# Two mixers reordered and the opening rebuilt in a two-block transformer kernel

## What is computed

```python
h = rmsnorm(x, mix_norm[l])
z = h @ w_in[l]
q, k, v, f_logit, gate_in, rec_in = jnp.split(z, split_points, axis=-1)
log_f = jax.nn.log_sigmoid(f_logit.astype(jnp.float32) + b_forget[l].astype(jnp.float32))
att = forgetting_attention(...)   # softmax(q k^T * scale + c_q - c_k, causal) v, c = cumsum(log_f)
rec = causal_depthwise_conv(rec_in, conv_w[l], conv_b[l])
rec = rg_lru(rec, w_a[l], b_a[l], w_x[l], b_x[l], lru_lambda[l])
lru_out = rec * jax.nn.gelu(gate_in, approximate=True)
x = x + jnp.concatenate([att, lru_out], axis=-1) @ w_out[l]
```

```python
q, k, v, g = jnp.split(x @ w_in, [H * dk, 2 * H * dk, 2 * H * dk + H * dv], axis=-1)
q = retention_rotate(...); k = retention_rotate(...) * (dk ** -0.5)
y = retention_chunkwise(q, k, v)          # ((q k^T) * decay mask) v, over chunks
y = head_rms(y).reshape(B, T, H * dv)
return (jax.nn.silu(g) * y).astype(x.dtype) @ w_out
```

## Time and profile before

| | |
|---|---|
| median of 3 runs | 2901.12 us (2900.29 to 2904.52) |
| the profiled execution's own time | 2903.57 us |
| its span | 2901.6 us |
| mean granted TensorE clock | 0.974 |
| TensorE busy | 2732.4 us, 94% |
| VectorE, ScalarE, GpSimd busy | 61%, 49%, 4% |

### The profile page before, as it was taken

One profiled execution on the slowest core, in us unless ns is written; L12 is line 12 of the kernel. 1 busy time (PEld: TensorE's weight loads), 2 busy tenths in 40 slices (PEclk: granted clock), 3 DMA queues, 4 the chain that ended last, 5 costly groups with the idle time before them and its releaser, 6 DMA issues.

```text
span 2901.6 us, 47985 instructions
## 1 busy us (share of the span) xinstructions
PE 2732.4 (94%) x19842; PEld 2461.7 (85%) x19842; DVE 1766.3 (61%) x2117; ACT 1421.8 (49%) x1872; POOL 115.2 (4%) x187
## 2 busy tenths in 40 slices
PE   4789999989999999997998999999999999999999
PEld 4669999978898888887897888889978888888887
DVE  3445588865655656568765656556546665555655
ACT  3435467644545445457323545445335455454544
POOL 0000000000000000000211000000000000000000
PEclk9889999999999999999999999999999999999999
DMA  5207599945543555553301555555535555543453
GB/s 168 73 5 249 176 320 358 332 158 188 169 150 121 199 188 182 188 174 105 129 4 42 193 190 188 189 189 179 178 116 181 188 167 192 193 147 129 167 189 130
DMA packets 377581, 491.96 MB, mean 170 GB/s; under 512 B 18872, under 2 KB 337760, under 8 KB 377408
## 3 DMA queue, kind: packets, MB, share of 16 engines
q1 hardware_dynamic: 365280, 479.23, 49.7%
q0 software_dynamic: 2192, 7.73, 0.8%
q10 hardware_dynamic: 9936, 2.47, 0.4%
HBM read 488.35 MB, written 1.05 MB: 169 GB/s over the span
## 4 chain that ended last, share of the span: by engine, by line
PE 87%; DVE 6%; ACT 4%; issue 1%; POOL 1%; ACTq 1%; DMA 0%; POOLq 0%; DVEq 0%
PE bank L348 20%; PE bank L347 11%; PE bank L327 9%; PE bank L328 9%; PE bank L329 9%; PE acc L327 7%; PE acc L329 7%; PE acc L328 7%; PE bank L2592 1%; ACT w_hi L292 1%; PE acc L588 1%; DVE X L499 1%; DVE w_lo L297 1%; ACTq L874 1%; PE bank L2569 1%
## 5 line engine op out<-in xcount | busy, mean ns | idle before, releaser
L297 DVE TENSOR_TENSOR w_lo<-raw,w_hi 128x2048 fp32r<-128x2048 f32 x360 | 824.1, 2292 | 536.8 <-ACT w_hi L292 536.4
L292 ACT ACTIVATE w_hi<-raw 128x2048 fp32r<-128x2048 f32 x360 | 687.9, 1911 | 269.0 <-PE acc L329 234.3
L348 PE MATMUL bank<-act_both,w_hi 128*128 128x512 f32 x2560 | 654.6, 392 | 0.0
L348 PEld LDWEIGHTS bank<-act_both,w_hi 128*128 128x128 f32 x2560 | 465.2, 189 | 82.8
L347 PEld LDWEIGHTS bank<-act_both,w_lo 128*128 128x128 f32 x2560 | 349.2, 190 | 25.0
L327 PE MATMUL acc<-w_hi,mix_hi 128*128 128x512 f32 x928 | 364.4, 393 | 2.3 <-DVE mix_lo L3017 1.2
L329 PE MATMUL acc<-w_hi,mix_lo 128*128 128x512 f32 x928 | 362.5, 391 | 0.0
L328 PE MATMUL acc<-w_lo,mix_hi 128*128 128x512 f32 x928 | 362.3, 390 | 0.0
L347 PE MATMUL bank<-act_both,w_lo 128*128 128x256 f32 x2560 | 357.0, 282 | 0.0
L722 ACT ACTIVATE scratch<-bank 128x256 f32<-128x256 f32 x320 | 122.2, 385 | 429.2 <-PE bank L348 422.8
L327 PE MATMUL bank<-act_both,w_hi 128*128 128x256 f32 x1032 | 298.5, 289 | 21.0 <-DVE act_both L2844 8.4
(11 more groups left out here) (501 smaller groups left out, 3889.9 us busy)
## 6 DMA issues: line engine op xcount, KB each, us to landing
raw<-in_ffn_w_gu SPq DMA_DIRECT2D x176, 1024.0 KB, 5.1
raw<-in_ffn_w_down SPq DMA_DIRECT2D x88, 1024.0 KB, 4.9
raw<-in_ml_w_in SPq DMA_DIRECT2D x24, 1024.0 KB, 5.3
raw<-in_rt_w_in SPq DMA_DIRECT2D x24, 1024.0 KB, 5.1
raw<-in_w_up SPq DMA_DIRECT2D x20, 1024.0 KB, 7.7
raw<-in_w_gate SPq DMA_DIRECT2D x19, 1024.0 KB, 7.1
raw<-in_w_down SPq DMA_DIRECT2D x18, 1024.0 KB, 6.8
moe_raw<-in_w_down SPq DMA_DIRECT2D x14, 1024.0 KB, 6.9
```

Source lines behind the costliest of these rows:

```text
L292: act.activation(w_hi[0:rows, slot, 0:size], raw[0:rows, slot, 0:size], ACT.Copy).then_inc(hi_made, 1)
L297: dve.tensor_tensor(w_lo[0:rows, slot, 0:size], raw[0:rows, slot, 0:size], w_hi[0:rows, slot, 0:size].bitcast(F32), ALU.subtract).then_inc ...
L348: return pe.matmul(bank[b][:, :], w_hi[:, slot, w], act_both[:, k, :], start=k == 0, stop=k == KT - 1)
```

## The change

The opening: the constants are loaded in two pieces (the identity first). Of the vectors ScalarE's queue loads only `mix_norm`, which TensorE turns alone. The other vectors and the forget columns go to SyncE's queue behind the first three panels, the narrow weights and biases to GpSimd's queue behind the first norm. The splits of the first three panels move into the norm (`between`). GpSimd, not VectorE, clears `qz` (and `kz`).

The first mixer: panels come in the order v, rec, gate, q, k, and the output panels in the order 2, 3, 0, 1 (the recurrence's rows first). The forget columns are 24 products with a 72-row left side, the cumulative sum is a scan on VectorE, and both q and k carry it in unused rows of `qz` and `kz`, so that the product L986 and `cT` go away. The reciprocal is replaced by `a*a + 1` times the tanh. The scores write to the four `acc` banks, and `probs` has four buffers. The gates, the recurrence and the heads stand between panels.

Retention: the scores of all heads stand behind panel g0, the y and turns between the panels g1 to g7.

The core of the diff (TensorE's order in both mixers, the opening, and the parts of ScalarE's and VectorE's programs that wait for each other):

```diff
-            act.dma_start(con[:, :], consts).then_inc(consts_loaded, 16)
-            act.wait_ge(setup_dve, 2)
-            for dst, src in small_loads:
-                act.dma_start(dst, src).then_inc(small_loaded, 16)
-            act.wait_ge(small_loaded, 16 * len(small_loads))
-            act.activation(narrow_hi[:, :, :], narrow[:, :, :], ACT.Copy).then_inc(setup_act, 1)
-            for p in range(RING):
-                act_split(act, p, 1, None)
+            act.dma_start(con[:, 0:P], consts[:, 0:P]).then_inc(consts_loaded, 16)
+            act.dma_start(*vec_loads[0]).then_inc(mix_loaded, 16)
+            act.dma_start(con[:, P:], consts[:, P:]).then_inc(consts_loaded, 16)
+            act.wait_ge(cleared, 1)
+            act.activation(silu_out[:, 0, 0:32], exponent[:, :], ACT.Square)
 
...
-            dve.memset(exponent[:, :], -0.5).then_inc(setup_dve, 1)
-            dve.memset(rows_in[:, VEC_TILES - 1, :], 0.0).then_inc(setup_dve, 1)
-            dve.wait_ge(small_loaded, 16 * len(small_loads))
-            dve.wait_ge(setup_act, 1)
-            dve.tensor_tensor(narrow_lo[:, :, :], narrow[:, :, :], narrow_hi[:, :, :].bitcast(F32),
-                              ALU.subtract).then_inc(setup_dve, 1)
-            dve.wait_ge(setup_pe, 1)
-            dve.tensor_copy(vecs[:, :], acc[0][:, 0:VEC_TILES * P]).then_inc(setup_dve, 1)
-            for p in range(RING):
-                dve_split(dve, p, p)
+            dve.memset(exponent[:, :], -0.5).then_inc(cleared, 1)
+            dve.memset(rows_in[:, VEC_TILES - 1, :], 0.0).then_inc(cleared, 1)
+            dve.memset(f_w[:, :, :], 0.0).then_inc(cleared, 1)
+            dve.wait_ge(mix_turned, 1)
+            dve.tensor_copy(vecs[:, 0:MIX_ROWS], acc[3][:, 0:MIX_ROWS]).then_inc(mix_ready, 1)
+            dve.wait_ge(mix_ready, 1)
...
-            pe.wait_ge(consts_loaded, 16)
-            pe.wait_ge(small_loaded, 16 * len(small_loads))
-            pe.wait_ge(setup_dve, 2)
-            for j in range(VEC_TILES):
-                last = pe.transpose(acc[0][:, j * P:j * P + P], rows_in[:, j, :], ident)
-            last.then_inc(setup_pe, 1)
...
+            pe.wait_ge(consts_loaded, 32)
+            pe.wait_ge(mix_loaded, 16)
+            pe.matmul(acc[3][:, 0:MIX_ROWS], rows_in[0:MIX_ROWS, 0, :], ident[0:MIX_ROWS, 0:MIX_ROWS], start=True,
+                      stop=True).then_inc(mix_turned, 1)
+            pe.wait_ge(mix_ready, 1)
...
+                if j == RING:
+                    sp.wait_ge(cleared, 3)
+                    for dst, src in vec_loads[1:]:
+                        sp.dma_start(dst, src).then_inc(vec_loaded, 16)
+                    for dst, src in f_loads:
+                        sp.dma_start(dst, src).then_inc(f_loaded, 16)
                 sp_panel(sp, p, p % RING, [(col_view(p % RING), w[:, :, at:at + PW])])
...
+            att_pool.wait(pool, "k_cleared")
+            pool_cross(pool, c)
...
+            for dst, src in narrow_loads:
+                pool.dma_start(dst, src).then_inc(narrow_loaded, 16)
...
+                if h >= 4:
+                    att_act.wait(pe, ("exp", h - 4))
+                for t, cols, at in ((1, T, 0), (0, P, T)):
+                    pe.matmul(acc[h % 4][:, at:at + cols], qz[:, h, t * P:t * P + P], kz[:, h, 0:cols], start=True, stop=False)
+                    last = pe.matmul(acc[h % 4][:, at + cols - P:at + cols], ident, C("neg_qk"), start=False, stop=True)
...
+            project("rec", 0)
+            b = result("f")
...
+            project("rec", 1)
+            project("gate", 0)
+            project("gate", 1)
+            for j in range(4):
...
+                att_dve.wait(pe, ("conv", j))
...
+            project("q", 0)
+            project("k", 0)
+            project("q", 1)
+            for h in range(4):
+                scores(h)
+            project("k", 1)
+            turn(0)
+            turn(1)
+            wait_evacuated(pe, N["v", 0])
+            wait_evacuated(pe, N["v", 1])
+            values(0)
+            for h in range(4, 8):
+                scores(h)
+            turn(2)
+            turn(3)
+            values(1)
+            turn(4)
+            turn(5)
+            values(2)
+            out_rows(0)
+            turn(6)
+            turn(7)
+            values(3)
+            out_rows(1)
...
+            projected("gate", 1)
+            act.wait_ge(narrow_loaded, 16 * len(narrow_loads))
+            act.activation(narrow_hi[:, :, :], narrow[:, :, :], ACT.Copy).then_inc(narrow_high, 1)
+            act.wait_ge(narrow_low, 1)
...
+            att_act.done(act.activation(lru_t[:, :, :], lru_t[:, :, :], ACT.Sqrt), "sqrt")
+            projected("q", 1)
+            for h in range(4):
+                exps(h)
+            lru_high(0)
+            lru_high(1)
+            projected("k", 1)
+            turned_copy(0)
+            turned_copy(1)
+            exps(4)
+            high(0)
+            turned_copy(2)
+            exps(5)
+            turned_copy(3)
+            high(1)
+            exps(6)
+            exps(7)
+            turned_copy(4)
+            turned_copy(5)
+            high(2)
+            act_split(act, (c.p + 13) % RING, loads(c.p + 13), E["out", 0])
+            turned_copy(6)
+            turned_copy(7)
+            high(3)
...
-                own(dve.tensor_scalar(lru_r[:, :, :], lru_t[:, :, :], 1.0, None, ALU.add))
-                own(dve.reciprocal(lru_r[:, :, :], lru_r[:, :, :]))
...
+            att_act.wait(dve, ("powers", 3))
+            own(dve.tensor_tensor(lru_r[:, :, :], lru_a[:, :, :], lru_a[:, :, :], ALU.mult))
+            att_dve.done(dve.scalar_tensor_tensor(lru_t[:, :, :], lru_r[:, :, :], 1.0, lru_t[:, :, :], ALU.add, ALU.mult),
+                         "square")
+            ahead("q", 0)
+            ahead("k", 0)
+            att_act.wait(dve, "sqrt")
+            own(dve.tensor_tensor(lru_i[:, :, :], lru_i[:, :, :], lru_t[:, :, :], ALU.mult))
+            for j in range(4):
+                last = dve.tensor_tensor_scan(lru_r[:, j, :], lru_a[:, j, :], lru_i[:, j, :], 0.0, ALU.mult, ALU.add)
+            att_dve.done(last, "u")
...
+            for j in range(2, 8):
+                project("v", j)
+            for j in range(8):
+                project("q", j)
+            project("g", 0)
+            for h in range(4):
+                scores(h)
+            project("g", 1)
+            for j in range(8):
+                wait_evacuated(pe, N["v", j])
+            retained(0)
+            project("g", 2)
+            retained(1)
+            turn(0)
+            project("g", 3)
+            retained(2)
+            turn(1)
+            project("g", 4)
+            retained(3)
+            project("g", 5)
+            turn(2)
+            project("g", 6)
+            project("g", 7)
+            turn(3)
```

More of the change, by code:

```diff
@@ L465, in act_cross @@
                 x_sum(0)
+            if between:
+                between(0)
             if norm:
@@ new lines, in dve_att @@
+            ahead("q", 0)
[5 more added lines that the diff above has]
+            att_dve.done(last, "u")
+            att_dve.wait(dve, "u")
+            for j in range(2):
+                wait_evacuated(dve, N["gate", j])
+                lru_out(j)
@@ L2221, in pe_rt, with turn @@
+            def turn(h):
+                rt_dve.wait(pe, f"scaled{h}")
+                for i in range(2):
+                    b = result("turn", h, i)
                     for m in range(2):
```

908 lines of the change are left out of this document (516 added, 392 removed).

## The result

The changed kernel takes 2850.31 us (median of 4 runs, 2847.51 to 2854.70), the kernel before 2902.82 on the same chip (4 runs). The ratio is 0.9821, with a 95% interval of 0.9804 to 0.9838: 1.8% faster, some 52 us. The profiled execution took 2848.55 us (span 2846.8), 55.0 less than that of before. The forecast was 2845.

What follows compares the result with a forecast made beforehand. TensorE, busy 94% of the span, was taken as the bound, so gains come from its idle or slow time: 48.3 us through the first mixer (opening's 24.7 included) plus 7.5 in retention, 55.8, giving 2845 us; range 2830 to 2862 (8 in 10).

Steps and rivals of the forecast that it cites:

- The opening: Kernel start: first norm's diagonal moves from 38.03 to 13.2 us, the second panel's product from 47.8 to 23.1; gain 24.7 us.
- What was put at nothing: Opening: moved vector, forget, panel 3 and narrow loads, and GpSimd's clearing of `qz` and `kz`, were taken to cost nothing.
- 1.9: First mixer: TensorE's wait for q0's bank, 5.3 us of ScalarE's work against 3.4 of gate products; 1.9 us.
- 7.2: First mixer: TensorE out of work from 93 us until the second turned copy near 100, before the first values; 7.2 us.
- 1.5: First mixer: wait because turned copies of heads 2 and 3 stand between the exponentials of heads 4 and 5; 1.5 us.
- 2.8: First mixer: wait because turned copies of heads 4 and 5 stand behind the exponentials of 6 and 7; 2.8 us.
- 2.0: First mixer: wait because turned copies of heads 6 and 7 stand behind the last split, which waits for the first output panel; 2.0 us.
- clock: First mixer: products at 1.2 GHz around one long wait and three short ones; taken at 3 us.
- Retention: Retention's heads: 6.4 us of TensorE idle time plus about 1 of slow clock go; gain 7.5, bounds 0 and 8.5.
- The rule on table changes: Skill's 1.38 us drain beside each 1.28 us ScalarE table load; four changes before the first exponential add 5.5 us, sum 2851.
- the slower one: Rival, chance 0.02: GpSimd's narrow loads hold ScalarE before the gates, with 36 us free; slower than 2901, 2908 at 14 us each.
- Relays overlap better: Rival, chance 0.17: ScalarE and VectorE overlap, so half of the 15.4 us of mixer waits and no clock loss; 2834.

Runs made afterwards that it cites:

- e1: Changed kernel with ScalarE again issuing the vectors, forget and narrow weights itself and waiting for them before the first norm's squares; 2863.66 us, ratio 0.9859.
- e7: Changed kernel with the first three panels' splits again ahead of the first norm on both engines, small loads as changed; 2857.89 us, ratio 0.9841.
- e4: Changed kernel with, on ScalarE alone, turned copies of heads 0 and 1 ahead of k1's copy and split and the recurrence's copies; 2845.41 us, ratio 0.9793.
- e10: The changed kernel itself run again, nothing edited, on the same chip and in the same rounds; 2848.01 us, ratio 0.9812 against the kernel before.
- e8: Changed kernel with GpSimd's ten narrow loads made three times, each behind the last's landing, ScalarE and VectorE waiting for the third; 2857.15 us, ratio 0.9831.
- e5: Changed kernel with the first mixer's heads taken ahead of what doesn't feed them, on VectorE, ScalarE and TensorE; 2838.86 us, ratio 0.9769.
- e6: Changed kernel with heads first on three engines, plus narrow weights split behind rec 1 and q1's split behind the gates; 2836.66 us, ratio 0.9755.
- e2: Changed kernel with the five retention programs of the kernel before; 2857.78 us, ratio 0.9835.
- e3: Changed kernel with ScalarE splitting the narrow weights behind panel rec 1 and doing q1's split behind the four gates; 2844.27 us, ratio 0.9792.

## Why the prediction was right, and where it was off

- **The opening**: 24.7 us predicted, 47.79 to 23.07 measured, 24.7. The second panel's product starts when VectorE's low half is made, at 23.0; I had 23.1. One premise was wrong and cost nothing: the first half's products, which I had at the slow clock, follow every 0.12 us from 17.4 on. e1 and e7 show that the loads' wait and the splits ahead of the norm are two conditions, of 14.6 and 8.8 us.
- **What was put at nothing**: right. TensorE doesn't wait between 23 and 59 us. The allowance of 3 us for a narrow load was too much: four took 3.50. GpSimd's clearing cost nothing either; the root came at 13.5.
- **The first mixer's waits**: 15.4 predicted, 12.9 measured (1.76 of q0's bank, then 0.38 + 0.67 + 5.52 + 0.60 + 2.07 + 1.88). Against the terms: 1.9 was 1.76; 7.2 was 6.57; 1.5 was 0.60; 2.8 was 2.07; 2.0 was 1.88. All five stand where the orders put them, the third below the 1 us that I had as the least. I read the 2.5 us too much as ScalarE and VectorE overlapping a little more than end to end; no run separates it. The *clock* was taken at 3, and cost about 3.7: some 1.4 at 65 us (between 65.0 and 68.3 the products follow every 0.21 us in place of 0.12), and 2.3 between 100.2 and 106.2, where the same work took 3.7 us in e4. From the second panel's product to the mixer's end there are 118.3 us; less waits and clock that leaves 101.7 of work, for which I had 100.2. Most of the 1.5 can be read as restarts behind waits, as under retention: the last product ahead of a wait is drawn 0.07 to 0.16 us longer than such products follow one another, and over the eight waits that is 1.2 (an estimate from the timeline). Errors of opposite sign made 141.7 meet 141.3. And the 190 from which I counted was the end of a window; the next norm's first product stood at 189.4 before, from which the forecast would have been 47.7 and not 48.3. No run puts the old mixer back: its 23.3 us are read from the two traces, and what the new order, the missing product with `cT`, the reciprocal, the forget columns and the banks each give is not shown.
- **Retention**: the term that was mis-sized. 7.5 predicted with a bound of 8.5; 9.2 from the sine on in every trace. The idle time is 6.4; the clock is not 1 but about 1.8 (the last turn 1.79 us for 1.04, and the first output products slow until 2143.9); another 1.0 is a remainder, and most of it can be read as idle time that the wait column doesn't hold, since a matmul's end is modelled and the tail of the last product ahead of a wait counts as busy. The Trainium skill has this too ("Perfetto Trace Analysis", "Tensor Engine Instruction (MATMUL, LD_WEIGHTS)": the end of a TensorE instruction is estimated, not measured). The five waits of the stage before each stand behind a product drawn 0.16 us longer than such products follow one another (0.27 for 0.11, 0.59 for 0.43), which makes 0.8; this is an estimate, no run measures a tail. The mistake was to set an upper bound at idle plus slow time, as if the column were complete. No transfer, split or bank stood in the way: from the sine on the stage has no wait at all.
- **Outside the two stages**: I had written that the prediction would be wrong if the rest changed by over 2 us. It did: from the first mixer to retention the changed kernel took 3.7 us longer, and behind retention 1.3 less. That test was too narrow, for the same program varies by 7.3 us there among the variants. Of the 3.7, 2.7 lie in the stage of the experts (410.98 for 408.32 us from diagonal to diagonal), which takes 408.64 to 411.04 in the variants. Whether a part belongs to the change stays open: the trace of before is a single one, and up to the sine it lies 1.4 below the fastest variant.
- **The sum**: 55.8 predicted; 48.0 + 9.2 - 2.4 = 54.8 in the traces (54.8 at the last diagonal too), 52.5 in the medians of the result, 57.6 in e10's rounds. The rule on table changes that was weighed and set aside would have given 2851, closer to the median by chance: the changes stay at 1.28 us with the next operation right behind, as at 81.92, where the square root starts at 83.22.
- **The rivals**: e8 shows that the slower one had its mechanism right; its threshold, a total past 2901, was not tried, and the room was 32.8 us (27.80 to 60.58) where I had 36. The loads hold ScalarE one for one past their cover, and the cover is some 22 us: landed by 38.8 (the last issue's end at 35.6 and the 3.2 that e8 waited for it), split at 60.6. "Relays overlap better" was partly true, as the waits show.

## What to carry to other kernels

Ahead of a relay between engines, look at each engine's program for what stands in front of the relay's next step without feeding it: a split, a scan, a copy for later. Moving such work on one engine alone mostly moves the wait (e4: 5.5 and 0.3 us became 1.3 and 2.9, and the end came 1.1 earlier); moved on all three, the same work ended 12 to 13 us earlier (e5). When a blocking load is taken from the start, look for what stands behind it in the same program: here that was more than a third of the opening's gain. And read small edits at a milestone close behind them, not in the total.

## What the runs showed of the hardware

- TensorE's granted clock after a short wait is not a property of the program. Behind the same wait of 1.76 us, with the same gate products ahead of it, it fell to 1.2 GHz in one trace and stayed at 2.4 in six; behind the 2.0 us wait it fell in e6 and stayed in e5. Behind the wait of 5.52 us it was down to 1.2 GHz in all seven traces that have it (the changed kernel, e1, e2, e3, e7, e8, e10); only how soon it rose again differed. Behind the wait of 2.07 us it fell in five of these seven (e1, e2, e3, e7, e8). So this long wait cost its length and slow products every time, the shorter ones cost them sometimes. The Trainium skill says that the count of slow products at a kernel's start varies from run to run ("TensorE: Matmul & The Clock Gate", "What's actually happening"). These traces show the same in the middle of a kernel, worth 1.4 us behind q0's wait (65 to 68 us) and 1.6 in e6 against e5.
- Four narrow loads of 1024 pieces took GpSimd 3.50 us to issue, and ScalarE's hardware queue 5.05 in e1, beside the weight panels, with 3.76 for the one ahead of them (GpSimd: 0.92). For these five GpSimd's software queue was the quicker one here, 4.4 us for 8.8. For the next two loads of 1024 pieces it was not (1.76 us for 1.24 in e1, behind the landing of the first three weight panels by 19.4).
